# The dense experts' gate multiply on GpSimd instead of VectorE in a PEER expert stage

## What is computed

```python
def blk(args):
    xx, ii, ww = args
    u = jnp.take(pu, ii, axis=0)
    act = jax.nn.gelu(jnp.einsum('md,mkd->mk', xx, u), approximate=False)
    vv = jnp.take(pv, ii, axis=0)
    return jnp.einsum('mk,mkd->md', (act * ww).astype(xx.dtype), vv)
```

## Time and profile before

| | us |
|---|---|
| median of 3 runs | 5053.77 (5053.18 to 5062.45) |
| the profiled execution | 5051.28 |
| its span in the trace | 5049.4 |
| expert stage, from TensorE's first score to the end | 2987.2 to 5049.4 |
| a plain unit (number 13) | 56.60 |
| a unit with a sample routing behind it (number 14) | 68.33 |
| a unit with a tile's finish behind it (number 15) | 65.02 |

### The profile page before, as it was taken

The page is one execution under the profiler, slowest core; times in us unless marked ns, Lnnn a source line. Parts: engine busy times, 40 slices in busy tenths (PEclk is TensorE's granted clock), DMA queues, the critical chain, the costliest instruction groups (busy, mean ns, idle before and its releaser), DMA issues. The chain is left out here.

```text
span 5049.4 us, 80491 instructions
## 1 busy us (share of the span) xinstructions
PE 4346.1 (86%) x30920; PEld 2976.9 (59%) x30920; DVE 3328.2 (66%) x6528; ACT 1124.7 (22%) x2258; POOL 1677.7 (33%) x1412
## 2 busy tenths in 40 slices
PE   6999997875888887997988759999989899989970
PEld 6999996654777775653978634443434344434430
DVE  4232322445666661112997749999999999999998
ACT  2000001334555552124233320111100101111101
POOL 0000000001212210000143446666666566666666
PEclk9999998577999998998999879999999999999985
DMA  5422223211011014114022269999999999999987
GB/s 209 168 96 93 93 93 122 79 62 63 26 42 32 26 30 170 73 51 159 26 84 86 77 214 393 374 386 341 384 352 402 334 400 356 387 345 389 370 336 296
DMA packets 350603, 1012.43 MB, mean 201 GB/s; under 512 B 39116, under 2 KB 123020, under 8 KB 344760
## 3 DMA queue, kind: packets, MB, share of 16 engines
q0 software_dynamic: 156672, 570.49, 29.0%
q1 hardware_dynamic: 193592, 437.38, 23.9%
HBM read 903.76 MB, written 103.99 MB: 200 GB/s over the span
## 5 line engine op out<-in xcount | busy, mean ns | idle before, releaser
L2778 PE MATMUL peer_v_b<-peer_vt,peer_mix 128*128 128x512 f32 x2048 | 943.1, 615 | 123.8 <-DVE peer_mix L2615 80.0
L2766 PE MATMUL peer_s_b<-dense_hT_d,peer_ut 128*128 128x512 f32 x2048 | 901.0, 593 | 38.3 <-DMA peer_G2s<-mod 38.3
L2550 POOL DMA_INDIRECT peer_ring<-in_peer_v,peer_idx x544 | 712.6, 1310 | 290.1 <-issue 160.6
L2778 PEld LDWEIGHTS peer_v_b<-peer_vt,peer_mix 128*128 128x128 f32 x2048 | 402.0, 198 | 649.2 <-issue 495.9
L2544 POOL DMA_INDIRECT peer_ring<-in_peer_u,peer_idx x544 | 596.6, 1097 | 477.7 <-DVE peer_acc L2667 231.0
L2766 PEld LDWEIGHTS peer_s_b<-dense_hT_d,peer_ut 128*128 128x128 f32 x2048 | 389.7, 190 | 529.0 <-issue 490.4
L1524 POOL TENSOR_TENSOR rw_An<-rw_abT,rw_join 128x256 f32<-128x256 f32 x160 | 134.5, 847 | 1650.5 <-DVE rw_abT L1437 1316.2
L2667 DVE SCALAR_TENSOR_TENSOR peer_acc<-peer_ring,peer_coef,peer_acc 128x1024 f32<-128x1024 f32 x534 | 653.7, 1279 | 0.0
L2704 DVE CUSTOM_DVE_ANT_0 peer_ring<-peer_ring,peer_h 128x1024 f32<-128x1024 f32 x544 | 637.5, 1220 | 2.0 <-DVE peer_h L2681 1.0
L57 PE MATMUL proj_acc<-proj_hT_high,proj_w_low 128*128 128x352 f32 x1584 | 513.8, 324 | 16.7 <-DVEq L401 16.7
L58 PE MATMUL proj_acc<-proj_hT_low,proj_w_high 128*128 128x352 f32 x1584 | 508.6, 321 | 0.0
(11 more groups left out here) (424 smaller groups left out, 6531.6 us busy)
## 6 DMA issues: line engine op xcount, KB each, us to landing
peer_ut<-in_peer_ut SPq DMA_DIRECT2D x128, 512.0 KB, 8.1
peer_vt<-in_peer_v SPq DMA_DIRECT2D x128, 512.0 KB, 8.9
pT<-proj_o SPq DMA_DIRECT2D x66, 528.0 KB, 2.9
front_w<-in_w_in SPq DMA_DIRECT2D x66, 512.0 KB, 3.7
G<-route_G SPq DMA_DIRECT2D x32, 1024.0 KB, 9.3
peer_gt<-G SPq DMA_DIRECT2D x64, 512.0 KB, 7.2
proj_w_ada<-in_w_ada SPq DMA_DIRECT2D x16, 1024.0 KB, 6.1
peer_ring<-in_peer_u,peer_idx POOLq DMA_INDIRECT x544, 11.9
```

The source lines that it names most:

```text
L2550: pool.indirect_dma_start(out=ring[:, k, :], out_offset=None, in_=t["peer_v"], in_offset=bass.IndirectOffsetOnAxis(ap=idx[U % 2][:, k:k + ...
L2766: last = pe.matmul(s_b[:, n % 3, :], ut[:, n % UT, k, :], hT_d[:, k, :], start=(k == 0), stop=(k == KD - 1))
L2778: last = pe.matmul(v_b[:, m % 4, :], mix[:, part % 2, e, tokens], vt[:, part % 2, e, cols], start=(e == 0), stop=(e == PART - 1))
```

## The change

`mixes(n)` is written out on POOL instead of VectorE, with the same three waits: for gelu, for the load of G, for the sums that free the buffer. Each unit's four stand behind the v gathers 3 and 11 of the unit and the u gathers 3 and 11 of the next one; the first part's four stand behind the u gathers 3, 7, 11 and 15 of unit 0. `dense(U)` on VectorE keeps its places and hands out the adds alone.

```diff
             def _(pool):
+                def mixes(n):
+                    part = n // PART
+                    pool.wait_ge(gelued, n + 1)
+                    pool.wait_ge(gt_in[n // 2 % 2], 16 * (n // 4 + 1))
+                    if part >= 2:
+                        pool.wait_ge(o_summed, OUTS * (part - 1))
+                    by_half = lambda ap: ap.rearrange("p (h c) -> p h c", c=HALF)
+                    pool.tensor_tensor(by_half(mix[:, part % 2, n % PART, :]), by_half(gelu[:, n % 2, :]), gt[:, n // 2 % 2, :, n % 2, :],
+                                      ALU.mult).then_inc(mixed, 1)
+
                 for U in range(ALL):
...
+                        if U == 0 and k % 4 == 3:
+                            mixes(k // 4)
+                        if U and U < UNITS and k in (3, 11):
+                            mixes(PART * U + 2 + k // 8)
...
+                        if U + 1 < UNITS and k in (3, 11):
+                            mixes(PART * (U + 1) + k // 8)
...
                     for e in range(PART):
-                        n, m = PART * (U + 1) + e, OUTS * U + 2 * e
-                        if n < EXPERT_TILES:
-                            mixes(n)
+                        m = OUTS * U + 2 * e
                         yield
...
-                for n in range(PART):
-                    mixes(n)
```

More of the change, by code:

```diff
@@ L2606, in _ @@
                 dve.wait_ge(consts_in, 16 * CONSTS)
[L2608 to L2616, removed]
                 def adds(m):
```

## The result

The changed kernel takes 5093.01 us (median of 4 runs, 5083.57 to 5096.19) against 5054.03 for the kernel before on the same chip: 1.0085 of it, interval 1.0070 to 1.0100. That is 39 us slower, 33 above the forecast and 3 above the end of its range. The profiled execution took 5083.57, its span is 5081.7; the stages ahead of the change were some 10 us shorter in it, so I compare the expert stage alone: from TensorE's first score to the end 2062.2 us before and 2104.5 after, +42.4.

A forecast was written before the change was run, and what follows sets the result against it. VectorE's own instruction list was taken to set a unit's length. Terms 2 + 1 + 3 = +6 us on the profiled 5051.28 gave 5057.3; the median of the runs lies 2.5 higher, so 5060, range 5040 to 5090 (0.80).

The forecast's parts named there:

- B: Mix behind v gather 11 of a unit; predicted to fall into the routing searches and cost VectorE about nothing.
- D: Mix behind u gather 11 of the next unit; predicted to meet multiply-adds and end 0 to 2 us before the dots.
- Theory port: GpSimd's multiply shuts out a VectorE instruction for about its own length; the prediction took 0.83 us a meeting.
- late sums: TensorE's sums delayed by D: +1 us, bounds 0 and 20; as a rival 5080 to 5120, chance 0.22.
- A: Mix behind v gather 3 of a unit; predicted to stand among dots and cost VectorE 0.83 us.
- The start: First four mixes on POOL in unit 0, unit 1 starting 2 to 4 us later: +3, bounds 0 and 5.
- C: Mix behind u gather 3 of the next unit; predicted to stand among multiply-adds and cost VectorE 0.83 us.
- The exclusion: VectorE with two SBUF inputs and POOL's multiply block each other; rival without it: 5006, chance 0.04.
- 3 x 0.83 = 2.49 against 2.43: Three of four mixes meet a VectorE operation, against time given back: +0.06 us a unit, +2 over 31 units.
- The second rival, the dearer mix: Port held for all of POOL's 1.04 us: +0.69 a unit, +21, 5078 with the start; chance 0.18.
- The cheaper meetings: Rival: A or C lies behind an add, so two of four mixes cost: 5034, chance 0.09.
- The fit of D: Fourth sum ready 20.9 us after the first began, fourth add at 20.9: 0 to 1 us late in plain units.

The follow-up runs named there:

- the run with four extra multiplies on GpSimd a unit: Kernel before plus four 128x512 strided multiplies on GpSimd in each of 31 units, at the places of A, B, C and D, result unread: 1.0216, 5159.41 us.

## Why 1.28 and not 1.04

```diff
-                    by_half = lambda ap: ap.rearrange("p (h c) -> p h c", c=HALF)
-                    pool.tensor_tensor(by_half(mix[:, part % 2, n % PART, :]), by_half(gelu[:, n % 2, :]), gt[:, n // 2 % 2, :, n % 2, :],
+                    row = gt[:, n // 2 % 2, :, :, :].rearrange("p h e c -> p (h e c)")
+                    pool.tensor_tensor(mix[:, part % 2, n % PART, :], gelu[:, n % 2, :], row[:, n % 2 * 512:(n % 2 + 1) * 512],
```

> The changed kernel, but each multiply on GpSimd reads its 512 gate values as one row of the tile instead of eight strided pieces of 64; so it multiplies by other gate values, and the dense part's values differ. In the trace of the change a multiply lasts 1.28 us beside nothing and a dot that meets one 2.27 instead of 1.22, 1.05 lost. Theory 1, stride: the pieces make it 1.28 instead of the routing stage's 1.04. Then a multiply beside nothing is 1.04, a met dot or multiply-add loses 0.83, 0.22 less in each of 93 meetings (three in 31 units), and the meeting of B with the coefficients loses some 0.2 less too: 93 x 0.22 + 31 x 0.2 = 27 us back, 1.0032 of the kernel before, near 5066 to 5070. Theory 2, traffic: the memory is busy with the gathers' transfers and that makes it 1.28; then it stays 1.28 and the time stays at 1.0085 of before, 5093.

Measured: 1.0082 (1.0064 to 1.0099). The multiplies of the changed kernel and of this one:

```profile
L2545 POOL TENSOR_TENSOR peer_mix<-peer_gelu,peer_gt x128: 1268/1440/1502, 2994.6 to 4915.4; 128x512 f32<-128x512 f32 x128
L2545 POOL TENSOR_TENSOR peer_mix<-peer_gelu,peer_gt x128: 1269/1440/1537, 3005.6 to 4925.5; 128x512 f32<-128x512 f32 x128
```

The pieces are not the reason. Theory 2, traffic, was left, and the next run tests it against the operands' shape: again four extra multiplies in the kernel before.

```diff
+                    by_cell = lambda ap: ap.rearrange("p (b c) -> p b c", c=P)
+                    pool.tensor_tensor(by_cell(spare[:, :]), by_cell(G2p[:, 0:512]),
+                                       G2p[:, 512:516].unsqueeze(2).broadcast_to([P, 4, P]), ALU.mult).then_inc(spared, 1)
```

> As the run with four extra multiplies on GpSimd a unit, but with the operands in the shape of the routing stage: one row of 512, and 4 values each spread over 128. Theory operands: a second input that is spread over its columns makes it 1.04 us beside nothing instead of 1.25, and each of three meetings a unit 0.83: 77 us and up to 10 for the coefficients, 1.015 to 1.017 of the kernel before, plain units near 59.2. Theory place (traffic, or standing directly behind a gather): it stays at 1.25, the time at 1.0216, plain units at 60.2.

Measured: 1.0172 (1.0156 to 1.0189), plain units 59.4. The multiplies, and a dot that meets one:

```profile
L2545 POOL TENSOR_TENSOR peer_spare<-peer_G2p x124: 1046/1214/1277, 3018.1 to 4960.8; 128x512 f32<-128x512 f32 x124
```
```profile
3841.62 2.05 DVE L2721 CUSTOM_DVE_ANT_0 peer_ring<-peer_ring,peer_h 128x1024 f32<-128x1024 f32 x1
```

In the same place, under the same transfers, the routing stage's operands give the routing stage's numbers: 1.05 beside nothing and 0.83 lost on a dot (0.78 on a multiply-add). So the earlier trace rows were read rightly, but for a multiply whose second input is four values spread over the columns; two full inputs take 0.20 to 0.23 us more.

## B, D and the moment of the meeting

```diff
-                        if U + 1 < UNITS and k in (3, 11):
+                        if U + 1 < UNITS and k in (3, 12):
```

> The changed kernel with B alone moved by one gather, from behind v gather 11 to behind v gather 12. In the trace of the change B ran from 3838.41 to 3839.69 in unit 13 and VectorE's product of the coefficients (128x16, two inputs) took 0.82 us instead of 0.17; over all units this product costs 8.3 us more, and the conversion behind it 1.7. Theory port: even that small two-input operation waits for the multiply to end; B starts 1.24 later, behind the product, and meets only operations with one input: 8 to 10 us back, 5083 to 5085, 1.0065 of before, and the product is back at 0.17. It could then meet the 128x256 sum of candidates instead and keep the loss. Rival: the product is longer because of something else in that place (ScalarE's gelu of the dots, the gathers); then it stays near 0.43 us in the mean and the time at 1.0085.

Measured: 1.0131 (1.0112 to 1.0150), 5112.38 us. The expectation fails: against the kernel before, the loss grew from 0.0085 to 0.0131, some 23 us more. The product costs 19.2 us more than before instead of 8.3, and the conversion behind it (L1985, one input) 13.5 more than before instead of 1.7. VectorE, then POOL, in unit 2's routing:

```profile
3160.77 0.17 DVE L2718 TENSOR_TENSOR peer_coef<-peer_act_d,peer_w 128x16 f32<-128x16 f32 x1 [0.22 <-DVE peer_pos L1970]
3160.98 1.86 DVE L1985 CAST peer_posf<-peer_pos 128x32 f32<-128x32 uint32 x1
```
```profile
3160.56 0.94 POOL L2564 DMA_INDIRECT peer_ring<-in_peer_v,peer_idx  x1 [0.31 <-issue]
3161.52 1.27 POOL L2545 TENSOR_TENSOR peer_mix<-peer_gelu,peer_gt 128x512 f32<-128x512 f32 x1
```

The conversion started 0.54 before the multiply's row does, while POOL's gather still ran, and ended with the multiply. In the kernel before, conversions that start at the same moment of a gather (0.40 to 0.43 in) with another gather behind it take 0.18. The rival that something else in that place holds the product falls too: every held product ends 0.04 behind the multiply.

Not all of the conversion's 1.86 is the multiply's, though. With a memset behind the gather (a run below) a conversion at that moment takes 0.54 and ends with the gather; with another gather behind, one that starts 0.1 later takes 0.42, again to the gather's end. VectorE and POOL in the run with memsets:

```profile
4746.62 0.54 DVE L1985 CAST peer_posf<-peer_pos 128x32 f32<-128x32 uint32 x1
...
4746.22 0.94 POOL L2562 DMA_INDIRECT peer_ring<-in_peer_v,peer_idx  x1 [0.30 <-issue]
4747.15 0.54 POOL L2544 MEMSET peer_spare<- 128x512 f32 x1
```

and, in the run with the four strided multiplies,

```profile
3239.94 0.42 DVE L1985 CAST peer_posf<-peer_pos 128x32 f32<-128x32 uint32 x1
...
3239.40 0.98 POOL L2563 DMA_INDIRECT peer_ring<-in_peer_v,peer_idx  x1 [0.16 <-issue]
```

So the end of a gather holds a conversion by itself, and the multiply behind it goes on holding it. What a multiply does ahead of its own row is read from instructions that a gather's end does not hold, dots and multiply-adds, in the next run.

```diff
-                        if U == 0 and k % 4 == 3:
-                            mixes(k // 4)
-                        if U and U < UNITS and k in (3, 11):
-                            mixes(PART * U + 2 + k // 8)
+                        if U and U < UNITS and k in (3, 7):
+                            mixes(PART * U + 2 + k // 7)
...
+                for n in range(PART):
+                    mixes(n)
```

> The run with the first four multiplies back on VectorE, and D moved by four gathers, from behind u gather 11 to behind u gather 7, some 5 us earlier. Theory late sums: after unit 0, VectorE waits 8 us in that run before adds of units 4, 9, 17, 20, 25 and 28, and TensorE's list starts as late as D; with D 5 us earlier these waits go: 1.0053 of the kernel before instead of 1.0069, units 9, 17 and 25 near 58 instead of 58.9 to 60.2, the meetings' cost unchanged. Rival: the waits come from something that D does not move (the loads of the experts); then they stay, and the time too.

Measured: 1.0098 (1.0081 to 1.0115). The adds of units 1 to 31, the run with D at its old place and then this one:

```profile
L2638 DVE TENSOR_TENSOR peer_acc_d<-peer_acc_d,peer_v_b 128x512 f32<-128x512 f32 x248 | 168.3, 679 | 8.6 <-PE peer_v_b L2790 8.4
```
```profile
L2638 DVE TENSOR_TENSOR peer_acc_d<-peer_acc_d,peer_v_b 128x512 f32<-128x512 f32 x248 | 168.4, 679 | 0.0
```

Their waits are gone, so the late sums need D's place; what else they need follows with the prediction's steps. But the time rose, from 1.0069 to 1.0098. VectorE's multiply-adds that meet D in unit 13, and POOL beside them:

```profile
3866.92 5.21 DVE L2679 SCALAR_TENSOR_TENSOR peer_acc<-peer_ring,peer_coef,peer_acc 128x1024 f32<-128x1024 f32 x3
```
```profile
3866.39 0.95 POOL L2554 DMA_INDIRECT peer_ring<-in_peer_u,peer_idx  x1 [0.30 <-issue]
3867.36 1.27 POOL L2545 TENSOR_TENSOR peer_mix<-peer_gelu,peer_gt 128x512 f32<-128x512 f32 x1
```

They take 5.21 instead of 3.67: 1.54 lost, since the first of them started 0.44 before D's row, behind an add. Where POOL's multiply had to wait for a running instruction first, as A and D in the changed kernel (their rows are 1.45 and 1.49), a meeting costs 1.0. So the price of this multiply goes by the moment at which VectorE's instruction begins: 0.46 late in the multiply, 1.0 behind a running instruction, 1.2 to 1.7 ahead of the multiply's row. This lead is not one of every operation. Of the instructions that start 0.4 ahead of the row, dots lose 1.55 to a multiply of 512 columns and 0.25 to a copy; a memset takes nothing, and a multiply of 64 columns waits itself, with a row of 1.00 instead of 0.33:

```profile
3321.69 1.21 DVE L2719 CUSTOM_DVE_ANT_0 peer_ring<-peer_ring,peer_h 128x1024 f32<-128x1024 f32 x1
```
```profile
3322.07 1.00 POOL L2544 TENSOR_TENSOR peer_spare<-peer_G2p 128x64 f32<-128x64 f32 x1
```

Why the long multiply is ahead of its row and the short one is not stays open.

## The start

```diff
-                        if U == 0 and k % 4 == 3:
-                            mixes(k // 4)
...
+                for n in range(PART):
+                    mixes(n)
```

The added lines stand on VectorE, ahead of unit 0.

> The changed kernel with only the first part's four multiplies back on VectorE, ahead of unit 0, as before. Theory start: in the trace of the change the time from the stage's first score to unit 1's first dot is 98.1 us against 91.3, so 6.8 us come back: about 5086, 1.007 of before, with plain units still 57.9. Rival: the start's loss only anticipates a wait that TensorE's sums bring later in any case; then unit 1 is 6.8 earlier, later units are longer by as much, and the time stays at 1.0085, 5093.

Measured: 1.0069 (1.0054 to 1.0084); unit 1's first dot comes 92.4 after the first score, not 98.1, and plain units stay near 57.9. The intervals of the two kernels overlap, so the reading rests on the traces: the stage is 2098.9 instead of 2104.5. The start theory holds: 5.7 us of the change's loss are the first four, and they don't come back later.

## Which work of GpSimd collides

Both runs are the kernel before with another extra operation at the four places; first a copy, then a memset.

```diff
+                    pool.tensor_copy(spare[:, 0:512], G2p[:, 0:512]).then_inc(spared, 1)
```

> As the run with four extra multiplies on GpSimd a unit, but each extra operation is a copy of 512 values: one SBUF input instead of two. Its length is in no row; by the two shapes of the multiply, 1.05 with a spread operand and 1.25 with a full one, an estimate of 0.85 with none. Theory port by reading: it collides as the multiply does, and a met dot or multiply-add loses its length less 0.22 to 0.27, 0.6: 90 x 0.6 = 54 us and up to 7 for the coefficients, 1.011 to 1.012. Rival: only an operation with two inputs on both sides collides; then 1.000 to 1.002.

Measured: 1.0063 (1.0042 to 1.0084). The copy lasts 0.61 beside nothing, not the 0.85 estimated, and holds 97 dots and multiply-adds for 0.35 to 0.40 each, its length less some 0.25: the port theory with the length mis-sized.

```diff
+                    pool.memset(spare[:, 0:512], 0.0).then_inc(spared, 1)
```

> As the run with four extra multiplies on GpSimd a unit, but each extra operation only writes: 512 zeros. Theory port by reading: nothing that reads, nothing that is met: 1.000 to 1.002 of the kernel before, dots and multiply-adds at 1.22 and 1.28. Rival, any operation of GpSimd takes the port for its length: its length less 0.2 to 0.3 in 90 meetings, over 1.005 if it is longer than 0.6.

Measured: 1.0001 (0.9990 to 1.0013). The memset lasts 0.54, nearly as long as the copy; dots and multiply-adds keep their lengths. The rival would have cost 0.29 x 90 = 26 us, 1.005, outside the interval. It is reading SBUF that collides. The Trainium skill, page "SBUF — State Buffer", section "Who interferes with whom", says just this of a VectorE instruction with two SBUF inputs, and lists `cast` and `tensor_scalar` among those that can take the shared pair, under conditions on their operands: the conversion of one input that ended with the multiply after 1.86 us agrees.

## The place

```diff
+                        if U + 1 < UNITS and k == 11:
+                            mixes(PART * (U + 1) + 1)
...
-                        if n < EXPERT_TILES:
+                        if e in (0, 2, 3) and n < EXPERT_TILES:
                             mixes(n)
```

> B alone on GpSimd, behind v gather 11 as in the change; A, C, D and the first four on VectorE at their places of before. Theory port: VectorE gives back 0.61 us a unit, 19 us in 31 units, and loses between nothing and 0.65 a unit at the coefficients' product: 0.996 to 1.000 of the kernel before; without A in front of it on GpSimd, B stands earlier and should miss the product: 0.9963. Rival, gathers and sums: not faster, 1.000 or more.

Measured: 0.9963 (0.9949 to 0.9976), 5029.67 us; plain units 56.1, the product at 0.17, no instruction held. In the time 0.6 a unit comes back; in the trace a plain unit is 0.52 shorter, 0.60 for the mix less 0.06 ahead of C, which now waits for B's end.

```diff
+                        if U + 1 < UNITS:
+                            for e, behind in enumerate((10, 10, 13)):
+                                if k == behind:
+                                    mixes(PART * (U + 1) + e)
...
-                        if n < EXPERT_TILES:
+                        if e in (3,) and n < EXPERT_TILES:
                             mixes(n)
```

> A, B and C on GpSimd, D and the first part's four on VectorE at their places of before; A and B stand behind v gather 10, C behind v gather 13, so that all three fall into the stretch of some 12 us in which VectorE searches for the next experts, mostly with operations of one input. Theory port: they meet next to nothing, VectorE gives back 3 x 0.61 = 1.83 us in each of 31 units, 57 us, plain units 54.8; TensorE's list of 8 x 6.92 = 55.4 may keep plain units there, then 20 x 0.6 = 12 us less: 45 to 57 us, 0.989 to 0.991 of the kernel before. One coefficient product met in each unit would cost 0.65 x 31 = 20 of it. Rival, gathers and sums: a multiply on GpSimd costs by what it delays behind it, wherever it stands; then this kernel is not faster than before by over 0.3%, 0.997 or more. The second of the two multiplies behind v gather 10 follows a multiply and not a gather: if 1.28 us is the price of the place behind a gather, it is near 1.04; if it is the traffic or the operands, it is 1.28 too.

Measured: 0.9908 (0.9891 to 0.9925), 5008.73 us, faster than both kernels. Windows of units 13 and 14:

```profile
3790.03:3844.93 54.90, 54.90 (x130) 24.29 (x129) 52.50 (x96) 5.57 (x9) 41.76 (x36) 1.00 1.01 403
3844.93:3911.63 66.70, 66.70 (x157) 29.55 (x156) 61.78 (x135) 9.03 (x14) 43.32 (x37) 1.00 1.02 409
```
```profile
L2546 POOL TENSOR_TENSOR peer_mix<-peer_gelu,peer_gt x93: 1265/1277/1449, 3046.7 to 4817.6; 128x512 f32<-128x512 f32 x93
```

One coefficient product is held in all, and four scalings of the found positions (one input, 128x16) that cost 3.4. TensorE is now busy for the whole plain unit, but it is not the bound that the expectation allowed for: VectorE's adds wait 0.4 us in the whole stage, and a unit's length is still VectorE's list, 56.60 less 1.82 for three mixes plus 0.15 for a conversion at the end of a gather. The same three multiplies that cost time in the changed kernel bring 43 us here, so what they delay on POOL costs next to nothing. The second of the two multiplies behind v gather 10 takes 1.27 as well: standing behind a gather is not what makes it 1.28.

```profile
3757.65 1.27 POOL L2546 TENSOR_TENSOR peer_mix<-peer_gelu,peer_gt 128x512 f32<-128x512 f32 x1
```

## The prediction, step by step

**Right:** VectorE's own list is the length of a unit, and a mix on it is worth the 0.61 forecast (0.60 in the trace; one a unit gave 0.0037 of the time, 19 us, by itself). The exclusion, and that adds don't take part in it. That the gathers keep up: dots waited for them in unit 0 alone. That D comes close to the first dots: the sums of unit 14 now start 1.4 before them, released by POOL.

```profile
3869.03 7.13 PE L2780 MATMUL peer_v_b<-peer_vt,peer_mix 128*128 128x512 f32 x16 [2.73 <-POOL peer_mix L2545]
```

**Wrong, the term "3 x 0.83 = 2.49 against 2.43".** This is the largest miss. 0.83 was the price of a multiply with a spread operand; with two full ones a whole meeting is 1.00 to 1.06. In units 1 to 30 dots, multiply-adds and the four scalings lost 88.2, 2.94 a unit, against 72.7 that the mixes gave back: +15.5 where +2 was forecast. The second rival, the dearer mix, had the right mechanism, with the wrong reason (the strided halves) and a price that fits by chance: the 1.04 it took for the whole of a shorter multiply is what is left of 1.28. The cheaper meetings were there as well, ten dots at 0.46. No row that I picked had the right shape, but the trace of before has one: in an earlier stage POOL multiplies two inputs that both change from column to column, 256 and 64 columns wide.

```profile
L1524 POOL TENSOR_TENSOR rw_An<-rw_abT,rw_join x160: 718/728/1952, 1200.8 to 1912.0; 128x256 f32<-128x256 f32 x160
L1524 POOL TENSOR_TENSOR rw_An<-rw_abT_smp,rw_join x8: 318/320/321, 1266.1 to 1915.2; 128x64 f32<-128x64 f32 x8
```

From 0.318 to 0.718 is 2.08 ns a column, and carried on to 512 columns that makes an estimate of 1.25: the length of 1.24 to 1.28 could have been read before the change.

**Wrong, "B falls into the routing searches, which read one input".** The searches do, but between them stands a product of 128x16 with two inputs, 0.17 us long and so in none of the rows that I picked. It was held in 13 units and the conversion behind it, which does read one input, in one, 10 us in all where the forecast had nothing. A short instruction waits as long as a long one.

**Too small, late sums:** +1 forecast, 7.5 measured, inside the bounds of 0 and 20. The fit of D is right where TensorE's clock stayed up, and misses where it did not. The first pair of sums of units 12 and 13, and the windows from its start to the score behind it:

```profile
3752.95 9.58 PE L2780 MATMUL peer_v_b<-peer_vt,peer_mix 128*128 128x512 f32 x16 [13.62 <-POOL peer_mix L2545]
3811.10 7.13 PE L2780 MATMUL peer_v_b<-peer_vt,peer_mix 128*128 128x512 f32 x16 [0.51 <-POOL peer_mix L2545]
```
```profile
3752.95:3762.36 9.41, 9.41 (x16) 4.06 (x17) 9.34 (x17) 0.00 (x0) 7.95 (x5) 0.74 1.01 409
3811.10:3818.07 6.97, 6.97 (x17) 3.14 (x18) 6.90 (x12) 0.12 (x1) 5.96 (x4) 1.00 1.02 418
```

Both begin 1.40 ahead of the unit's first dot. In unit 13 the fourth sum is there 20.87 after the first began, the 20.9 of the prediction, and no add waits. In unit 12 TensorE had been idle for 13.62 us, part of the pair ran at the lower level, 1.2 GHz (granted clock 0.74), the fourth sum is there after 23.31, and the adds wait 0.6. The six units whose early adds wait (9, 12, 17, 20, 25 and 28) all begin their sums so, after 7.8 to 13.6 us of idle TensorE (units 4, 8, 16 and 24 do too, and their sums still come in time); in unit 1 the sums begin as late against the first dot as in 9, 17 and 25, but at a clock of 1.00, and no add waits. The clock's price stood in no term of the prediction. That it makes the late sums is a comparison of units; no run held the clock fixed.

**Too small, the start:** +3 forecast, 6.8 measured, above its bound of 5. The stage's first score and first pair of sums on TensorE, and the windows of the scores before and now and of that pair:

```profile
2977.16 37.52 PE L2768 MATMUL peer_s_b<-dense_hT_d,peer_ut 128*128 128x512 f32 x80 [37.40 <-DMA peer_G2s<-mod]
3017.41 8.71 PE L2780 MATMUL peer_v_b<-peer_vt,peer_mix 128*128 128x512 f32 x16 [2.73 <-POOL peer_mix L2545]
```
```profile
2987.24:3023.47 36.23, 36.23 (x80) 15.99 (x81) 16.70 (x50) 4.07 (x7) 18.48 (x18) 0.95 0.67 257
2977.16:3014.60 37.44, 37.44 (x80) 16.20 (x80) 19.39 (x50) 4.08 (x7) 20.99 (x18) 0.92 0.70 255
3017.41:3026.10 8.69, 8.69 (x17) 3.93 (x18) 3.04 (x5) 0.00 (x0) 7.19 (x7) 0.82 1.03 419
```

The pair starts 40.25 after the first score, in the earlier trace rows 36.23: 4.0 later. The wait for the fourth mix is 2.73 of that, inside the 1.4 to 3.4 expected. The rest is the five scores, 37.4 instead of 36.2 at a clock of 0.92 instead of 0.95; that need not be the change's, since in the run with B alone, whose start is that of before, they take 37.3 too. The pair also lasts 8.71 instead of 7.03. After the 2.73 us of idle TensorE its granted clock is 0.82: its first products start 0.85 to 1.0 us apart, those after the fourth 0.43, so the first ran at the lower of the two levels, 1.2 GHz. That price, 1.7 us, stood in no term of mine. It is not the price of every such wait: the sums of unit 14 above also follow 2.73 us of idle TensorE and take 7.13 at a clock of 1.00. Wait and clock make 4.4 of the 5.7 that the run with the first four on VectorE gave back.

With the measured sizes the sum is 15.5 + 10 + 7.5 + 6.8 = 39.8 where the forecast had 2 + 0 + 1 + 3 = 6 and the stage has 42.4. No single miss leaves the range, all four together do, by 3 us. They stand on one side because the price of a meeting, B and the late sums had each been taken at the low end, and because the rivals were priced one at a time: a dearer mix that meets something in all four places is 4 x 1.04 - 2.43 = 1.73 a unit, 54 us, and was no rival.

## What to carry to other kernels

Work that is moved from VectorE to GpSimd is paid by what it meets, not by its own length: put it where VectorE runs instructions with one input or with PSUM, and look through that stretch for every short instruction with two SBUF inputs, conversions and scalings too. Take a duration from a row only if the operands have the same shape, a spread one being shorter than a full one; two widths of one operation give a line to carry on. Where several terms are each taken at the kind end of their bounds, the sum is not the likeliest value.

## What the hardware showed that was not expected

- A multiply of 512 columns on GpSimd behind a gather shuts out VectorE up to some 0.5 us before its own row starts: three multiply-adds took 5.21 instead of 3.67, and a dot that starts 0.4 ahead of the row loses 1.55. The Trainium skill, "SBUF — State Buffer", section "SBUF: two separate sides", has the lock held for the whole instruction; here it was held for longer than the instruction's row. A multiply of 64 columns has no such lead.
- The end of a gather holds a conversion that starts in it until the gather ends: 0.42 us instead of 0.18, with no multiply near.
- The length of a multiply on GpSimd goes by columns and by operands: 0.33 us for 64 columns, 1.25 for 512 with two full inputs, 1.05 with one spread; strided pieces and rows take the same. Between 64 and 512 columns that is 2.06 ns a column, with 0.19 us ahead of the first column, which the estimate of 1.11 in the prediction left out. The "GPSIMD Engine Reference" of the Trainium skill, section 3.1, has 2.6 cycles an element at 1.2 GHz; the slope here agrees nearly, at 2.5.
- GpSimd's memset of 0.54 us costs VectorE nothing; a copy of 0.61 us costs 0.35 to 0.40 where it meets two SBUF inputs.
